# Linear attention's first head pair prepared inside neighbourhood attention, decay products on four row groups

## The chip, the cores and the metric

One core of a Trainium2 chip runs one program. The metric is the device time of one execution in microseconds (us). A second, profiled execution gives the rows below.

## What is computed

A first block of two layers over 2048 latent tokens and 256 context tokens (D = 1024), then a second block. One layer of the first block, cut to what matters here:

```python
(fx, fgx, nqx, nkx, nvx, ngx, gqx, gkx, gvx, ggx, zfx, zbx) = split(hx @ w_in[l])     # the same for the context
na_x = neighbourhood_attention(nqx, nkx, nvx, nkc, nvc, rpb[l])                       # 6 heads of 64
log_a = log_sigmoid(z @ w_alpha + b_alpha) / 16          # z: 16 columns, once forward, once backward
# gla_scan, chunks of 64 tokens, 4 heads, dk = 48 (padded to 64), dv = 96, both directions:
b = cumsum(log_a in the chunk); b_end = b[last]
q_dec, k_dec = q * exp(b), k * exp(-b)
o = tril(q_dec @ k_dec.T) @ v + q_dec @ state
state = exp(b_end) * state + (k * exp(b_end - b)).T @ v
x = x + gate * (concat(four_x, na_x, gla_x, each times silu(gate columns)) @ w_out[l])
```

The modulation (shift, scale, gate) of a layer is `silu(c) @ w_ada[l] + b_ada[l]`, for the latent and the context tokens.

## The kernel before

The program is a row of phases; each ends in a barrier of all engines, and the waits inside one are semaphores written out by hand. A layer of the first block has these:

- `cm` (`norm_project_cm`): norm, transpose, and the projection of twelve 128-column chunks, channels on partitions. Its 60 blocks (a chunk times 512 tokens, the fifth of each chunk 256) are 24 TensorE (PE) matmuls each: every float32 product is made of three fp32r products (`matmul3`, L72 to L74). The blocks n = 10 to 29 of chunks 2 to 5 are rotated for position (`Rotation`): one product L238 on PE after the next block, three VectorE (DVE) operations L248, L249, L251. In layer 0 `Modulation` is spread over the same blocks: GpSimd (POOL) loads 64 weight tiles of 256 KB into three buffers, DVE multiplies them into a sum in 64 steps of two operations (L335, L337), and after each of eight groups of eight steps PE reduces the sum (`reduce`, L307 to L316), which it reaches in its own order ahead of a block, waiting for `acc_ok`. Group j starts at block 9 + 6j with two steps in each of four blocks.
- `tm` (`project_tm`): four column chunks of 512, 512, 384, 384 columns times 16 or 18 token tiles, tokens on partitions, 24 matmuls a tile, ScalarE (ACT) evicts each (L940). Inside it `DecaySums` makes log_a and its running sums in 20 units (5 token segments times 2 head pairs times 2 directions), one after every third tile: one PE product of 16 contraction rows into one PSUM bank (L783), four ACT activations, two DVE operations, a store. The next segment's ranks are loaded into `z` by SyncE (SP) after the fourth unit's store.
- `four` (Fourier mix), then `na` (`neighbourhood_phase`): 18 (layer 0) or 16 (layer 1) query tiles times 6 heads, so NU = 108 or 96 units. In loop turn n DVE does `softmax_max(n + 2)` (L1285) and `probs_out(n)` (L1302), ACT does `exps(n + 1)` (L1339), on odd n `values_out` (L1345), and `tb` copies of unit n (L1357, L1359). PE does per pair of units the scores (L1215), transposes (L1227, L1233), values (L1245) and one transpose back (L1255).
- `gla` (`gla_phase`): head pairs hh = 0 and 1. SP loads the pair's running sums of both directions, k, v and q. ACT makes the exponentials of the chunk ends (`eb`, L1611), of the keys (L1614) and of the queries (L1618), DVE multiplies (`keys_decayed` L1540, `keys_to_end` L1544, `queries_decayed` L1551), PE transposes the keys back (L1452), ACT evicts them (L1625), PE makes the state updates of batch i (`states`, L1474), DVE chains them (`chain`, L1568), and a loop over the token tiles follows (products L1491, mask L1578, outputs L1503 and L1511). DVE's order is fixed: all six `prepare(0, n)` come ahead of `chain(0, 0)`. Pair 1 is prepared inside the loop of pair 0.
- `out` (`out_phase`): the output projection. Its weights come into the four buffers `wo.buf`, which are the decayed queries and keys of pair 0 before.

## Time and the profile before

| | us |
|---|---|
| median of 3 runs | 4718.71 (4718.05 to 4732.49) |
| the profiled execution | 4721.0 |
| its span | 4719.2 |
| PE busy | 4208.3 (89%) |
| DVE busy | 2202.5 (47%) |
| ACT busy | 1482.8 (31%) |
| POOL busy | 465.4 (10%) |

Times in the profile count from the start of the span. A matmul's end is modelled, and the matmuls of one row overlap, so a busy PE need not be at its peak; PEclk is the clock that PE was granted, 1.00 for 2.4 GHz and 0.50 for 1.2 GHz. In brackets stands how long the engine sat idle before an instruction, and what ended that. A float32 product counts as two MATMUL instructions. Layer 0's phases lie at about 64 to 430 (cm), 430 to 829 (tm), 829 to 943 (four), 943 to 1220 (na), 1220 to 1396 (gla), layer 1's na ends and its gla begins at about 2729.

### The profile page before, as it was taken

What the parts mean: (1) busy time and instruction counts of PE and PEld (TensorE: products, weight loads), DVE (VectorE), ACT (ScalarE), POOL (GpSimd) and SP (SyncE); (2) the same over time, 40 slices, a digit from 0 to 9 for tenths busy, and PEclk for the clock granted to TensorE, in tenths of its full rate; (3) what the DMA queues carried; (4) which work ended last, traced back from release to release, by engine and by line L of the source; (5) the groups of instructions that cost most, each with busy time, mean ns of one, the idle gap of its engine ahead of it and who ended that gap; (6) DMA issues with size and microseconds to landing.
All of it is one profiled execution on the core that took longest, in us unless ns stands there. A gap on an engine that the chain in (4) does not pass through costs nothing. (4 is left out here: it accounts for less than half of the span.)

```text
span 4719.2 us, 67376 instructions
## 1 busy us (share of the span) xinstructions
PE 4208.3 (89%) x25867; PEld 3358.5 (71%) x25867; DVE 2202.5 (47%) x4748; ACT 1482.8 (31%) x3341; POOL 465.4 (10%) x497
## 2 busy tenths in 40 slices
PE   7999999799669899999979956959999989979799
PEld 4777789577457778778857745847777767758687
DVE  5553111266656553111126665853831256657554
ACT  4001333156412220144316631431111257641211
POOL 3111000200000030000020000031420000100100
PEclk9999999999759999999989976979999999989899
DMA  4343121710325442212180043532111123346321
GB/s 179 118 132 112 72 72 54 262 42 13 127 101 200 171 151 69 94 72 72 58 273 14 14 151 125 219 148 78 63 65 64 61 84 118 96 156 256 116 75 64
DMA packets 230291, 520.88 MB, mean 110 GB/s; under 512 B 46587, under 2 KB 100747, under 8 KB 220627
## 3 DMA queue, kind: packets, MB, share of 16 engines
q1 hardware_dynamic: 206068, 434.47, 25.9%
q0 software_dynamic: 23904, 82.11, 4.8%
q8 instruction: 207, 3.39, 0.3%
q14 instruction: 112, 0.91, 0.1%
HBM read 320.07 MB, written 196.43 MB: 109 GB/s over the span
## 5 line engine op out<-in xcount | busy, mean ns | idle before, releaser
L72 PE MATMUL tm_tacc<-tm_tw_hi,hT_hi 128*128 128x384 f32 (+1 forms) x1120 | 418.6, 374 | 1.6 <-POOL tm_tw_lo L916 1.6
L73 PE MATMUL tm_tacc<-tm_tw_lo,hT_hi 128*128 128x384 f32 (+1 forms) x1120 | 413.4, 369 | 0.0
L74 PE MATMUL tm_tacc<-tm_tw_hi,hT_lo 128*128 128x384 f32 (+1 forms) x1120 | 413.3, 369 | 0.0
L72 PE MATMUL tz_tacc<-tz_tw_hi,hT_hi 128*128 128x512 f32 x896 | 359.8, 402 | 24.4 <-DVE tz_tw_lo L892 12.8
L72 PE MATMUL cm_acc<-hT_hi,cm_wb_hi 128*128 128x512 f32 (+1 forms) x912 | 362.0, 397 | 0.0
L73 PE MATMUL tz_tacc<-tz_tw_lo,hT_hi 128*128 128x512 f32 x896 | 356.1, 397 | 0.0
L74 PE MATMUL tz_tacc<-tz_tw_hi,hT_lo 128*128 128x512 f32 x896 | 356.1, 397 | 0.0
L74 PE MATMUL cm_acc<-hT_hi,cm_wb_lo 128*128 128x512 f32 (+1 forms) x912 | 344.0, 377 | 0.0
L73 PE MATMUL cm_acc<-hT_lo,cm_wb_hi 128*128 128x512 f32 (+1 forms) x912 | 343.5, 377 | 0.0
L804 DVE SCALAR_TENSOR_TENSOR tm_ds<-tm_dg,tm_ds 128x512 f32<-128x512 f32 (+1 forms) x40 | 25.6, 639 | 531.8 <-ACT tm_ds L798 531.8
L72 PEld LDWEIGHTS tm_tacc<-tm_tw_hi,hT_hi 128*128 128x128 f32 x1120 | 213.6, 191 | 56.5 <-ACT tm_tz L940 23.2
L74 PEld LDWEIGHTS tm_tacc<-tm_tw_hi,hT_lo 128*128 128x128 f32 x1120 | 213.3, 190 | 25.4
L73 PEld LDWEIGHTS tm_tacc<-tm_tw_lo,hT_hi 128*128 128x128 f32 x1120 | 213.6, 191 | 24.2
L72 PEld LDWEIGHTS tz_tacc<-tz_tw_hi,hT_hi 128*128 128x128 f32 x896 | 169.3, 189 | 78.8 <-POOL tz_tw_lo L916 17.8
L940 ACT ACTIVATE tm_tz<-tm_tacc 128x384 f32<-128x384 f32 (+1 forms) x140 | 75.8, 541 | 461.4 <-PE tm_tacc L74 426.0
L72 PE MATMUL out_acc<-out_w_hi,out_mT_hi 128*128 128x512 f32 x544 | 215.6, 396 | 0.0
L74 PE MATMUL out_acc<-out_w_hi,out_mT_lo 128*128 128x512 f32 x544 | 212.7, 391 | 0.0
L73 PE MATMUL out_acc<-out_w_lo,out_mT_hi 128*128 128x512 f32 x544 | 212.5, 391 | 0.0
L72 PEld LDWEIGHTS cm_acc<-hT_hi,cm_wb_hi 128*128 128x128 f32 x912 | 173.2, 190 | 41.5 <-issue 11.5
L724 ACT ACTIVATE cm_zo<-cm_acc 128x512 f32<-128x512 f32 (+1 forms) x57 | 32.2, 564 | 542.6 <-PE cm_acc L74 542.6
L73 PEld LDWEIGHTS cm_acc<-hT_lo,cm_wb_hi 128*128 128x128 f32 x912 | 173.4, 190 | 37.6 <-issue 7.5
L74 PEld LDWEIGHTS tz_tacc<-tz_tw_hi,hT_lo 128*128 128x128 f32 x896 | 169.5, 189 | 41.2
(370 smaller groups left out, 8801.2 us busy)
## 6 DMA issues: line engine op xcount, KB each, us to landing
scr_z<-tz_tz SPq DMA_DIRECT2D x112, 256.0 KB, 2.0
scr_zcm<-cm_zo SPq DMA_DIRECT2D x96, 256.0 KB, 2.0
scr_ztm<-tm_tz SPq DMA_DIRECT2D x68, 256.0 KB, 2.0
out_mx<-scr_mix SPq DMA_DIRECT2D x34, 512.0 KB, 3.6
out_gt<-scr_ztm SPq DMA_DIRECT2D x34, 512.0 KB, 4.5
scr_xres<-out_x POOLq DMA_DIRECT2D x34, 512.0 KB, 4.1
scr_z<-out_xn POOLq DMA_DIRECT2D x34, 512.0 KB, 4.7
cm_area<-in_w_ada POOLq DMA_DIRECT2D x64, 256.0 KB, 3.1
```

The source lines that it names most:

```text
L72: nc.tensor.matmul(out, ah, bh, start=start, stop=False)
L73: nc.tensor.matmul(out, ah, bl, start=False, stop=False)
L74: return nc.tensor.matmul(out, al, bh, start=False, stop=stop)
L724: act.activation(zo[n % 4][:, 0:b - a], acc[n % 4][:, 0:b - a], ACT.Copy).then_inc(ev_act, 1)
L804: nc.vector.scalar_tensor_tensor(s, g, 0.0, s, ALU.min, ALU.subtract)
L940: act.activation(zo[n % 3][:, 0:widths[c]], acc[n % 3][:, 0:widths[c]], funcs[c]).then_inc(ev, 1)
```

## The change

Four edits.

- A class `LinearInputs` (`pre`) holds, behind neighbourhood attention's own buffers, the four rows of pair 0, its k and q, `eb` and `ls`. SP loads them after the store of query tile 1. In the turns n = 24 onwards of `neighbourhood_phase` ACT makes one piece a turn (the chunk ends, then exponentials of 256 tokens), after `exps(n + 1)`; DVE multiplies the same piece two turns later, after `probs_out`. There are 38 pieces in layer 0 and 36 in layer 1.
- `gla_phase` no longer loads or prepares pair 0, except `keys_to_end(0, d)`, two DVE operations that now stand first. v is its first load, then the masks, then pair 1's four.
- `DecaySums` has ranks and weights on four row groups (partitions 0, 32, 64, 96) and four PSUM banks: the four products of a segment are issued together, once every fourth unit. The ranks of the next segment are loaded after the store of the first unit of a segment. All units move one tile later, so the first product is behind the first tile.
- `Modulation` starts at block 26 with a period of 4 blocks: three, three and two steps in blocks 27 + 4j, 28 + 4j and 29 + 4j; the reduction of group j stands ahead of block 31 + 4j (`reduced`, unchanged, asks for position 1 of the next period).

One more phase (`pre`) encloses the others, so one more barrier stands at a layer's end.

```diff
-        self.start, self.period = 9, 6
+        self.start, self.period = 26, 4
...
-        if p == 2 and 1 <= j <= self.NG:
+        if p == 1 and 1 <= j <= self.NG:
             self.row(dve, j - 1)
-        if 0 <= j < len(self.chunks) and p >= 2:
-            self.step(dve, j, 2 * p - 4)
-            self.step(dve, j, 2 * p - 3)
+        if 0 <= j < len(self.chunks) and p >= 1:
+            for k in range(3 * p - 3, min(3 * p, KC)):
+                self.step(dve, j, k)
...
-        self.z, self.wa, self.ba = P.sb("dz", [64, 512]), P.sb("dwa", [64, 256]), P.sb("dba", [128, 4])
+        self.z, self.wa, self.ba = P.sb("dz", [128, 512]), P.sb("dwa", [128, 128]), P.sb("dba", [128, 4])
...
-        self.bank = P.ps("dbank")
+        self.bank = [P.ps(f"dbank{j}") for j in range(4)]
...
-        self.at = {sum(tiles[:c]) + 3 * j: 5 * c + j for c in range(4) for j in range(5)}
+        self.at = {sum(tiles[:c]) + 3 * j + 1: 5 * c + j for c in range(4) for j in range(5)}
...
-            sp.wait_ge(self.g_mm, 4 * seg)
-        for d in range(2):
-            sp.dma_start(self.z[32 * d:32 * d + RANK, 0:w], rank_rows(self.io)[d, :, a:a + w]).then_inc(self.z_in, 16)
+            sp.wait_ge(self.g_mm, seg)
+        for j in range(4):
+            sp.dma_start(self.z[32 * j:32 * j + RANK, 0:w], rank_rows(self.io)[j % 2, :, a:a + w]).then_inc(self.z_in, 16)
...
-        if u % 4 == 3 and u < 19:
+        if u % 4 == 0 and u < 16:
...
     def pe(self, pe, u):
-        hh, d, a, w = self.place(u)
+        if u % 4:
+            return
         if u == 0:
-            pe.wait_ge(self.c_in, 48)
+            pe.wait_ge(self.c_in, 64)
         else:
             pe.wait_ge(self.g_ev, u)
-        pe.wait_ge(self.z_in, 32 * (u // 4 + 1))
-        self.nc.tensor.matmul(self.bank[:, 0:w], self.wa[32 * d:32 * d + RANK, hh * 128:(hh + 1) * 128],
-                              self.z[32 * d:32 * d + RANK, 0:w], start=True, stop=True).then_inc(self.g_mm, 1)
+        pe.wait_ge(self.z_in, 64 * (u // 4 + 1))
+        w = self.place(u)[3]
+        for j in range(4):
+            last = self.nc.tensor.matmul(self.bank[j][:, 0:w], self.wa[32 * j:32 * j + RANK, :], self.z[32 * j:32 * j + RANK, 0:w], start=True, stop=True)
+        last.then_inc(self.g_mm, 1)
...
-        act.wait_ge(self.g_mm, u + 1)
+        act.wait_ge(self.g_mm, u // 4 + 1)
...
-        act.activation(g, self.bank[:, 0:w], ACT.Identity, bias=self.ba[:, 2 * d + hh:2 * d + hh + 1]).then_inc(self.g_ev, 1)
+        act.activation(g, self.bank[u % 4][:, 0:w], ACT.Identity, bias=self.ba[:, 2 * d + hh:2 * d + hh + 1]).then_inc(self.g_ev, 1)
...
+                    if i == 2:
+                        pre.load(sp, io)
...
+                    if 0 <= n - first - 2 < len(pre.pieces):
+                        pre.dve(dve, n - first - 2)
...
+                    if 0 <= n - first < len(pre.pieces):
+                        pre.act(act, n - first)
...
-                for hh in range(2):
-                    sp.dma_start(qd[hh][0][:, :], decay_sums(io, hh, 0)).then_inc(b_in[hh][0], 16)
-                    sp.dma_start(k[hh][:, :], io["zcm"][10 + hh, :, :]).then_inc(k_in[hh], 16)
-                    sp.dma_start(qd[hh][1][:, :], decay_sums(io, hh, 1)).then_inc(b_in[hh][1], 16)
-                    if hh == 0:
-                        sp.dma_start(v[:, :, :], io["ztm"][:, 1024 + D_NA:TM].rearrange("(t p) c -> p t c", p=128)).then_inc(m["v_in"], 16)
-                    sp.dma_start(q[hh][:, 0:LQ], io["zcm"][8 + hh, :, 0:LQ]).then_inc(q_in[hh], 16)
-                    if hh == 0:
-                        for cc in range(2):
-                            sp.dma_start(mask[64 * cc:64 * cc + 64, :, :],
-                                         io["gla_mask"][64 * cc:64 * cc + 64, :, 64 * cc:64 * cc + 64]).then_inc(m["cst_in"], 16)
+                sp.dma_start(v[:, :, :], io["ztm"][:, 1024 + D_NA:TM].rearrange("(t p) c -> p t c", p=128)).then_inc(v_in, 16)
+                for cc in range(2):
+                    sp.dma_start(mask[64 * cc:64 * cc + 64, :, :],
+                                 io["gla_mask"][64 * cc:64 * cc + 64, :, 64 * cc:64 * cc + 64]).then_inc(m["cst_in"], 16)
+                sp.dma_start(qd[1][0][:, :], decay_sums(io, 1, 0)).then_inc(b_in[0], 16)
+                sp.dma_start(k[:, :], io["zcm"][11, :, :]).then_inc(k_in, 16)
+                sp.dma_start(qd[1][1][:, :], decay_sums(io, 1, 1)).then_inc(b_in[1], 16)
+                sp.dma_start(q[:, 0:LQ], io["zcm"][9, :, 0:LQ]).then_inc(q_in, 16)
...
-                    pe.wait_ge(m["qd_ok"], 2 * (hh + 1))
+                    if hh:
+                        pe.wait_ge(m["qd_ok"], 2)
...
-                nc.vector.memset(ls[:, :], math.log(GDK ** -0.5)).then_inc(m["ls_ok"], 1)
+                for d in range(2):
+                    keys_to_end(0, d)
...
-                for n in range(6):
-                    prepare(0, n)
+                dve.drain()
...
-                act.wait_ge(m["ls_ok"], 1)
-                exp_keys(0, 0)
-                exp_keys(0, 1)
-                exp_queries(0, 0)
                 keys_out(0, 0)
-                exp_queries(0, 1)
...
+class LinearInputs:
+    W = 256
+    def __init__(self, P, nc):
+        self.nc = nc
+        self.sums_in = [P.sem(f"sums{d}_in") for d in range(2)]
+        self.keys_in, self.queries_in, self.exp_ok, self.ls_ok = P.sem("keys_in"), P.sem("queries_in"), P.sem("exp_ok"), P.sem("ls_ok")
+    def place(self, P, LQ):
+        self.LQ = LQ
+        self.rows, self.eb, self.ls = self.behind(P)
+        self.k, self.q = [self.nc.alloc_sbuf_tensor(f"{P.name}_{n}0", [128, LT], F32, side="right") for n in "kq"]
+        self.pieces = []
+        for d in range(2):
+            self.pieces += [("ends", d, 0)] + [("keys", d, a) for a in range(0, LT, self.W)] + [("queries", d, a) for a in range(0, LQ, self.W)]
+    def behind(self, P):
+        right = lambda n, shape: self.nc.alloc_sbuf_tensor(f"{P.name}_{n}", shape, F32, side="right")
+        return [right(f"row{j}", [128, LT]) for j in range(4)], right("eb", [128, 2, 2, NCH]), right("ls", [128, 1])
+    def load(self, sp, io):
+        sp.dma_start(self.rows[0][:, :], decay_sums(io, 0, 0)).then_inc(self.sums_in[0], 16)
+        sp.dma_start(self.k[:, :], io["zcm"][10, :, :]).then_inc(self.keys_in, 16)
+        sp.dma_start(self.rows[1][:, :], decay_sums(io, 0, 1)).then_inc(self.sums_in[1], 16)
+        sp.dma_start(self.q[:, 0:self.LQ], io["zcm"][8, :, 0:self.LQ]).then_inc(self.queries_in, 16)
+    def act(self, act, j):
+        what, d, a = self.pieces[j]
+        b, e = self.rows[d], self.rows[2 + d]
+        if what == "ends":
+            act.wait_ge(self.sums_in[d], 16)
+            act.wait_ge(self.ls_ok, 1)
+            bc = b[:, :].rearrange("p (c t) -> p c t", t=CH)
+            act.activation(self.eb[:, 0, d, :], bc[:, :, CH - 1] if d == 0 else bc[:, :, 0], ACT.Exp, scale=1.0 / 16)
+            act.drain().then_inc(self.exp_ok, 1)
+        elif what == "keys":
+            act.activation(e[:, a:a + self.W], b[:, a:a + self.W], ACT.Exp, scale=-1.0 / 16)
+            act.drain().then_inc(self.exp_ok, 1)
+        else:
+            act.activation(b[:, a:a + self.W], b[:, a:a + self.W], ACT.Exp, scale=1.0 / 16, bias=self.ls[:, 0:1]).then_inc(self.exp_ok, 1)
+    def dve(self, dve, j):
+        what, d, a = self.pieces[j]
+        if what == "ends":
+            return
+        if j == 1:
+            dve.wait_ge(self.keys_in, 16)
+            dve.wait_ge(self.queries_in, 16)
+        dve.wait_ge(self.exp_ok, j + 1)
+        x, y = (self.rows[2 + d], self.k) if what == "keys" else (self.rows[d], self.q)
+        self.nc.vector.tensor_tensor(x[:, a:a + self.W], y[:, a:a + self.W], x[:, a:a + self.W], ALU.mult)
...
-        self.buf = [P.sb(f"buf{j}", [128, LT]) for j in range(4)]
+    def __init__(self, P, pre):
+        self.buf = pre.behind(P)[0]
...
+    with phase(nc, f"pre{l}") as Q:
+        pre = LinearInputs(Q, nc)
+        with phase(nc, f"nain{l}") as P:
+            na = Neighbourhood(P, last)
+            fourier_phase(nc, l, io, keep, na)
+            pre.place(P, LX if last else LT)
+            neighbourhood_phase(nc, l, io, keep, na, pre)
+        with phase(nc, f"wo{l}") as P:
+            wo = OutputWeights(P, pre)
+            gla_phase(nc, l, io, keep, wo, pre)
```

## Rows read from the trace of the kernel before

**Rows 1.** Busy time by phase, PE, PEld, DVE, ACT, POOL, granted clock, DMA share, GB/s.
```profile
437.00:841.00 404.00, 387.98 (x1784) 326.96 (x1783) 63.88 (x83) 148.35 (x202) 16.39 (x16) 0.97 0.21 77
943.00:1220.00 277.00, 266.60 (x2622) 193.97 (x2622) 177.76 (x400) 167.41 (x451) 0.00 (x0) 0.97 0.08 27
1220.00:1400.00 180.00, 114.15 (x1928) 98.19 (x1928) 109.60 (x303) 45.41 (x108) 0.00 (x0) 0.59 0.33 121
```

**Rows 2.** Timeline, layer 0, start of gla: start, duration, engine, instruction, [idle before].
```profile
1219.80 0.32 SPq L1419 DMA_DIRECT2D wo_buf<-scr_branch  x1
...
1226.20 0.26 ACT L1611 ACTIVATE gla_eb<-wo_buf 128x36 f32<-128x36 f32 x1 [10.98 <-DMA wo_buf<-scr_branch]
...
1231.63 2.56 DVE L1544 TENSOR_TENSOR gla_kd<-wo_buf,gla_eb 128x2304 f32<-128x2304 f32 x1
...
1234.25 4.10 PE L1452 MATMUL gla_bank<-ident,gla_kd 128*128 128x128 f32 x18 [18.65 <-DVE gla_kd L1544]
...
1244.00 3.53 PE L1474 MATMUL gla_bank<-gla_v,gla_kt 64*64 64x96 f32 x160 [0.53 <-ACT gla_kt L1625]
1244.33 5.03 DVE L1551 TENSOR_TENSOR wo_buf<-gla_q,wo_buf 128x2304 f32<-128x2304 f32 x2 [5.02 <-DMA gla_q<-scr_zcm]
...
1249.27 13.04 DVE L1568 SCALAR_TENSOR_TENSOR gla_S<-gla_S,gla_eb,gla_bank 128x96 f32<-128x96 f32 x40
...
1252.52 1.88 PE L1474 MATMUL gla_bank<-gla_v,gla_kt 64*64 64x96 f32 x40 [4.99 <-DVEq L1571]
```

**Rows 3.** Timeline, layer 1, start of gla.
```profile
2734.21 0.26 ACT L1611 ACTIVATE gla_eb<-wo_buf 128x36 f32<-128x36 f32 x1 [9.69 <-DMA wo_buf<-scr_branch]
...
2756.39 9.75 DVE L1568 SCALAR_TENSOR_TENSOR gla_S<-gla_S,gla_eb,gla_bank 128x96 f32<-128x96 f32 x30
```

**Rows 4.** ACT's groups by form in layer 0's na: busy, mean ns, idle before.
```profile
L1357 ACT ACTIVATE na_pt<-na_tpb 128x256 f32<-128x256 f32 x108 | 41.5, 384 | 86.8 <-PE na_tpb L1233 86.8
...
L1339 ACT ACTIVATE na_s<-na_s,na_st 128x256 f32<-128x256 f32 x12 | 6.0, 499 | 0.0
```

**Rows 5.** Timeline, layer 0's na, one pair of units.
```profile
1053.51 1.78 PE L1215 MATMUL na_sp<-nain_k,nain_q 64*128 64x512 f32 x12
1053.61 0.38 ACT L1357 ACTIVATE na_pt<-na_tpb 128x256 f32<-128x256 f32 x1 [0.63 <-PE na_tpb L1233]
...
1056.24 0.38 ACT L1357 ACTIVATE na_pt<-na_tpb 128x256 f32<-128x256 f32 x1 [1.12 <-PE na_tpb L1233]
```

**Rows 6.** Timeline of PE in tm, around one decay product.
```profile
509.72 0.40 PE L73 MATMUL tm_tacc<-tm_tw_lo,hT_hi 128*128 128x512 f32 x1
509.96 0.39 PE L74 MATMUL tm_tacc<-tm_tw_hi,hT_lo 128*128 128x512 f32 x1
510.39 1.09 PE L783 MATMUL tm_dbank<-tm_dz,tm_dwa 16*128 16x512 f32 x2
511.41 0.50 PE L72 MATMUL tm_tacc<-tm_tw_hi,hT_hi 128*128 128x512 f32 x1
```

**Rows 7.** The decay products' tile: instructions, duration min, median, max.
```profile
L783 PE MATMUL tm_dbank<-tm_dz,tm_dwa x80: 374/587/1189, 435.2 to 2325.9; 16*128 16x512 f32 x64, 16*128 16x256 f32 x16
```

**Rows 8.** Waits in tm, layer 0: us, times, longest.
```profile
PE tm_dbank L783 <- DMA tm_dz<-scr_branch: 12.4, 3, 8.0
```

**Rows 9.** Waits in cm, layer 0.
```profile
PE cm_msums L307 <- DVEq L341: 5.1, 3, 3.7
...
PE cm_ntp L238 <- DVE cm_zo L692: 3.3, 2, 2.5
```

**Rows 10.** Granted clock after two waits of PE, columns as in rows 1.
```profile
246.00:255.00 9.00, 6.56 (x14) 2.80 (x15) 4.23 (x7) 0.00 (x0) 0.00 (x0) 0.62 0.15 59
683.00:691.00 8.00, 7.53 (x21) 6.23 (x22) 0.00 (x0) 0.00 (x0) 0.00 (x0) 0.57 0.06 21
```

**Rows 11.** Timeline, DVE in cm, a modulation step that waited.
```profile
407.08 1.42 DVE L337 SCALAR_TENSOR_TENSOR cm_area<-cm_area,cs 128x512 f32<-128x512 f32 x2 [2.08 <-DMA cm_area<-in_w_ada]
```

**Rows 12.** DVE's groups in cm, the rotation's last operation.
```profile
L251 DVE TENSOR_TENSOR cm_zo<-cm_zo,cm_ntp 128x512 f32<-128x512 f32 x16 | 11.0, 688 | 1.2
```

More of the change, by code:

```diff
@@ L757, in ranks @@
         if seg:
-            sp.wait_ge(self.g_mm, 4 * seg)
-        for d in range(2):
-            sp.dma_start(self.z[32 * d:32 * d + RANK, 0:w], rank_rows(self.io)[d, :, a:a + w]).then_inc(self.z_in, 16)
+            sp.wait_ge(self.g_mm, seg)
+        for j in range(4):
+            sp.dma_start(self.z[32 * j:32 * j + RANK, 0:w], rank_rows(self.io)[j % 2, :, a:a + w]).then_inc(self.z_in, 16)
     def load(self, sp):
         l, io = self.l, self.io
-        sp.dma_start(self.wa[:, :], io["w_alpha"][l:l + 1, :, :].rearrange("a p n -> p (a n)")).then_inc(self.c_in, 16)
+        self.ranks(sp, 0)
+        for hh in range(2):
+            sp.dma_start(self.wa[64 * hh:64 * hh + 64, :], io["w_alpha"][l:l + 1, :, hh * 128:(hh + 1) * 128].rearrange("a p n -> p (a n)")).then_inc(self.c_in, 16)
         sp.dma_start(self.ba[:, :], io["b_alpha"][l:l + 1, :, :].rearrange("a p n -> p (a n)")).then_inc(self.c_in, 16)
         sp.dma_start(self.start[:, :], io["chunk_start"][:, 0:512]).then_inc(self.c_in, 16)
-        self.ranks(sp, 0)
     def store(self, sp, u):
@@ L1182, in neighbourhood_phase @@
         NPT = NA_H // 2
+        first = 4 * NA_H
         def key_tiles(i):
@@ L1374, in gla_phase @@
         mask = P.sb("mask", [128, 2, CH], I32)
-        ls = P.sb("ls", [128, 1])
-        q = [P.sb(f"q{j}", [128, LT]) for j in range(2)]
-        k = [P.sb(f"k{j}", [128, LT]) for j in range(2)]
+        ls = pre.ls
+        q, k = P.sb("q", [128, LT]), P.sb("k", [128, LT])
         v = P.sb("v", [128, NT, GH * GDV])
-        qd = [wo.buf[0:2], [P.sb(f"qd1{d}", [128, LT]) for d in range(2)]]
-        kd = [wo.buf[2:4], [P.sb(f"kd1{d}", [128, LT]) for d in range(2)]]
+        qd = [pre.rows[0:2], [P.sb(f"qd1{d}", [128, LT]) for d in range(2)]]
+        kd = [pre.rows[2:4], [P.sb(f"kd1{d}", [128, LT]) for d in range(2)]]
         kt = [P.sb(f"kt{d}", [128, NT, 128]) for d in range(2)]
         ke = [kd[1], [P.sb(f"ke{d}", [128, LT]) for d in range(2)]]
-        eb = P.sb("eb", [128, 2, 2, NCH])
+        eb = pre.eb
         S = P.sb("S", [128, 2, NCH, GDV])
@@ L1404, in steps_needed @@
             return max(order[0].index(2 * n + 1), order[1].index(2 * n))
-        names = ("cst_in", "v_in",
-                 "ls_ok", "exp_q", "exp_k", "qd_ok", "kte_ok", "kt_mm", "kt_ev", "u_mm", "s_ok", "a_mm", "a_ok", "o_mm", "o_ok")
+        names = ("cst_in",
+                 "exp_q", "exp_k", "qd_ok", "kte_ok", "kt_mm", "kt_ev", "u_mm", "s_ok", "a_mm", "a_ok", "o_mm", "o_ok")
         m = {n: P.sem(n) for n in names}
-        b_in = [[P.sem(f"b{hh}{d}_in") for d in range(2)] for hh in range(2)]
-        q_in, k_in = [[P.sem(f"{n}{hh}_in") for hh in range(2)] for n in ("q", "k")]
+        b_in = [P.sem(f"b{d}_in") for d in range(2)]
+        q_in, k_in, v_in = P.sem("q_in"), P.sem("k_in"), P.sem("v_in")
         o_out = [P.sem(f"o_out{j}") for j in range(2)]
@@ L1546, in keys_to_end, with queries_decayed, prepare @@
                                             eb[:, hh, d, :, None].to_broadcast([128, NCH, CH]), ALU.mult).then_inc(m["kte_ok"], 1)
-                def queries_decayed(hh, d):
-                    dve.wait_ge(m["exp_q"], 2 * hh + d + 1)
-                    dve.wait_ge(q_in[hh], 16)
-                    nc.vector.tensor_tensor(qd[hh][d][:, 0:LQ], q[hh][:, 0:LQ], qd[hh][d][:, 0:LQ], ALU.mult).then_inc(m["qd_ok"], 1)
-                def prepare(hh, n):
+                def queries_decayed(d):
+                    dve.wait_ge(m["exp_q"], d + 1)
+                    dve.wait_ge(q_in, 16)
+                    nc.vector.tensor_tensor(qd[1][d][:, 0:LQ], q[:, 0:LQ], qd[1][d][:, 0:LQ], ALU.mult).then_inc(m["qd_ok"], 1)
+                def prepare(n):
                     if n in (0, 2):
-                        keys_decayed(hh, n // 2)
+                        keys_decayed(n // 2)
                     elif n in (1, 3):
-                        keys_to_end(hh, n // 2)
+                        keys_to_end(1, n // 2)
                     elif n in (4, 5):
-                        queries_decayed(hh, n - 4)
+                        queries_decayed(n - 4)
                 def chain(hh, i):
@@ L1603, in _ @@
                         elif hh == 0:
-                            prepare(1, n - 3)
+                            prepare(n - 3)
             @block.scalar
@@ L2840, in first_layer @@
                            [512, 512, 384, 384], [ACT.Silu] * 2 + [ACT.Copy] * 2, tiles, decays=DecaySums(P, nc, l, io, tiles))
-    with phase(nc, f"nain{l}") as P:
-        na = Neighbourhood(P, last)
-        fourier_phase(nc, l, io, keep, na)
-        neighbourhood_phase(nc, l, io, keep, na)
-    with phase(nc, f"wo{l}") as P:
-        wo = OutputWeights(P)
-        gla_phase(nc, l, io, keep, wo)
-        out_phase(nc, l, io, keep, wo)
+    with phase(nc, f"pre{l}") as Q:
[8 more added lines that the diff above has]
+            gla_phase(nc, l, io, keep, wo, pre)
+            out_phase(nc, l, io, keep, wo)
 def program(nc, io):
```

21 lines of the change are left out of this document (10 added, 11 removed).

## The prediction

> **What bounds the kernel now.** I read the page first (PE busy nearly everywhere, the granted clock below full only in a few slices), then a table of busy time by phase, then timelines at the places that the diff touches, and the waits last. In the table [rows 1] three kinds of phase are to be seen. tm and na belong to PE: 388.0 busy of 404.0 us and 266.6 of 277.0, at a clock of 0.97. There, what PE no longer does is gained, and work of DVE or ACT costs nothing as long as PE doesn't wait for it. gla belongs to nobody: PE 114 and DVE 110 of 180 us, clock 0.59. That is a chain of waits, so its start has to be read instruction by instruction [rows 2]. SP issues the first load at 1219.80; ACT gets the running sums at 1226.20; DVE does keys (2.56 us an operation) for both directions and then waits 5.02 us for q, the last of the loads, at 1244.33, because its order puts both queries' multiplications ahead of the first chain. The chain, which everything behind it needs, starts at 1249.27, 29.5 us after the first load. PE had its state updates under way at 1244.00. Layer 1 does the same, with the chain at 2756.39 [rows 3].
>
> **The change, gla.** Of the head, what stays is: two `keys_to_end` (2 x 2.56), transposes, evictions, and v. DVE starts at once, so the second is done at 1219.9 + 5.1 = 1225.0; PE's transposes take 4.10 us for a direction [rows 2] at the low clock, so the keys are back at 1222.5 + 8.2 = 1230.7, evicted at about 1231.5. v is now the first load. Before, the sums of one direction (128 x 2304 x 4 bytes, 1152 KB) were there at 1226.20, and six more such pieces (k, the other sums, v as three, q) at 1244.33: 6912 KB in 18.1 us, 382 KB/us. v alone is 3456 KB, 2304 KB more than the first load was, so it lands at 1226.2 + 6.0 = 1232.2, and is what is late next. The first batch of updates is 40 of 160 instructions, 0.9 us at the pace of row 1244.00, 1.88 at that of row 1252.52 [rows 2]; I take 1.6 with the semaphore. The chain starts at 1234.0, 15.3 us earlier; in layer 1 at 2734.2 + 6.0 + 1.6 = 2741.8, 14.6 earlier. Pair 1 isn't in the way: its four loads follow v at 3.0 us each, done at about 1245, its exponentials 2 to 3 us behind, and DVE wants the first of them only in turn 3 of the loop, some 29 us after the chain's start. The masks, for which DVE waits ahead of the chain, are 64 KB behind v. Below, the gain is 12 us a layer, from the state updates themselves (1244.00 to 1232.2), above 16.5. I take **29 us** for both, a little less than 29.9.
>
> **na takes the work over.** ACT gets 38 and 36 pieces. The same engine's operation on 128 x 256 takes 384 ns (copy) and 499 ns (exponential) [rows 4]; the chunk ends 0.26 us each [rows 2]. In a pair of units ACT is idle 0.63 and 1.12 us ahead of its copies, and both waits are for PE [rows 5]; over the phase it is idle (277 - 167)/108 = 1.0 us a unit [rows 1]. A piece with its drain, 0.5 to 0.7, fits. DVE's part is 256/2304 of 2.56 us, 0.28, 0.35 with fixed cost; DVE is idle (277 - 178)/108 = 0.9 us a unit. Its tight place is `softmax_max` of the odd unit, for which the next scores wait. The loads, 4.7 MB at 382 KB/us, take 12 us and more and go out at about turn 15; a unit is 277/108 = 2.56 us, so turn 24 is 23 us later. They stand on SP's queue ahead of the store of query tile 2, whose buffer isn't wanted until tile 4, 12 units (31 us) on; no other SP work waits. So na's cost is **1 us**, from nothing to 0.4 us a piece (30 us) if the pieces come to stand in PE's way. Without the cover they would cost some 0.5 x 74 = 37.
>
> **tm, the decay products.** PE starts one matmul each 0.24 us; around the product the distance is 1.45 [rows 6], so one costs 1.21. Of the 20 a layer (80 instructions, 16 of them with 256 columns [rows 7]) the first stands ahead of the first tile, 15 are wide and four narrow (about 0.8): 18.2 + 3.2 = 21.4 us. The product also waits for its ranks: 12.4 us in three waits, 8.0 of which is the first [rows 8], where the weights' split is needed too and I count nothing. The two others, 4.4 us, go, since the ranks are loaded nine tiles earlier. Behind one of them PE's clock is 0.57 of full for 8 us, from 683 on [rows 10], the lower of its two levels for most of it: 0.43 x 8 = 3.4 us. Added are five groups. That products on different rows run together is seen in na: 832 columns for each of two heads take 1.78 us in 12 instructions [rows 5], where one of 512 columns alone takes 1.09 [rows 6]; one after the other would be 1664/512 x 1.09 = 3.5. For four groups of 32 rows there is no row. Below, a group costs what one product did, 1.21; above, three more behind it, 1.21 + 3 x 1.09 = 4.5. Nearest is the row of the pairs, so I take 1.5 (eight weight loads instead of two) and 1.0 for the narrow one: 7.0 a layer. Net 21.4 + 4.4 + 3.4 - 7.0 = 22.2, **44 us** for both. ACT and DVE do the same units at the same distance.
>
> The Trainium skill (TensorE: Matmul & The Clock Gate, the section on the measured speedup of packing) has four row tiles with 512 columns at 3.07 times, not four. By that, a group would take 4 x 1.09/3.07 = 1.42 where one takes 1.09, 0.33 more than the lower bound: 1.54 where I take 1.5, which changes the sum by less than 1 us. It is an estimate from that page; no run here shows it yet.
>
> **cm, the modulation.** Now PE waits 5.1 us for DVE's sums and 3.3 for evictions that stand behind modulation steps [rows 9], and the longest wait leaves a clock of 0.62 for 9 us [rows 10], 3.4: 11.8 us in all. After, the steps stand behind the rotation, but not wholly. Group 0 shares blocks 27 to 29 with it: from the end of block 27 and the rotation product behind it (1.2, like a decay product) DVE has three rotations of three operations of 0.69 [rows 12], eight steps of 1.5 (one is 1.42 and a drain [rows 11]) and an eviction: 1.2 + 6.2 + 12.0 + 0.7 = 20 us. PE has until the reduction three blocks of 24 matmuls at 0.24 (5.7, the narrow one 2.9, 5.7) and three rotation products, 18: a wait of 2. The last five steps of a group run in one go, 7.5 and 0.7, with waits for the weights of up to 2.08 [rows 11]; where one of the two blocks ahead of the reduction is narrow (groups 1, 5, 6), PE needs 8.6, so a wait of 1 each. Left are 5 us, the gain **7**; between -2, if these waits reach the 2 to 4 us behind which the clock falls, and 12.
>
> **Added beside.** One more barrier in each layer. A change of phase with two of them is what lies between ACT's last work in na and the load: 10.98 idle less 6.40 from the load's issue to its use, 4.6 [rows 2]. So one costs at most 4.6; I take 0.5, **1 us** for both. Three memsets of DVE and the constant for the queries lie in the shade.
>
> **Sum.** 44 + 29 + 7 - 1 - 1 = 78. The profiled execution took 4721.0 us, so 4643; it is 2.3 above the median of the runs shown, so 4641 there.
>
> **The rivals.**
> (1) The four products run one after another. For it: nothing here shows 32-row groups, and each product is two instructions on the same rows. Against it: the pairs in na. Four groups of 4.5 and one of 2.3 are 20.3 instead of 7.0 a layer, 27 in all: 4668.
> (2) The pieces get in PE's way in na. For it: ACT's program order is rigid, and the drain after a piece has no row of its own. Against: PE, not ACT, is waited for in both gaps. At 0.4 us for each of 74 pieces: 4641 + 29 = 4670.
> (3) The modulation's group sums come late. For it: five steps in a row with three buffers. At waits of 2 us or more in four groups, each followed by a low clock: 7 becomes -7, 4655.
> (4) gla's head is shorter but its gain is given back, because the loop's next wait (pair 1's exponentials, v behind other traffic) ends last. At half the 29: 4655.
> (5) Slower than before: the pieces let PE's clock fall. In na it is 0.97, and it falls elsewhere behind waits of 2.3 us [rows 10]. If PE waited so in the turns with pieces, 74 x 2.56 = 190 us would run at the lower level, up to 190 us more: some 4830. It decides from 78 + 14 = 92 of these 190 us on. Against: no wait of that length follows from pieces of 0.5.
>
> **Chances.** The forecast 0.56, rival 1 0.14, rival 2 0.11, rival 3 0.10, rival 4 0.06, rival 5 0.03. The forecast's own range comes from its bounds: all of them good (group 1.21, cm 12, gla 33, other waits of the first tile) is 4620; the range to 1 in 10 of rivals 1 and 2 ends at 4672. 0.3% is 14 us, which is what a measurement of this kernel can tell from no change. All but rival 5 and a piling up of 2, 1 and 3 are faster by more: faster 0.95, same 0.02, slower 0.03.
>
> **What would show it.** In gla, the first DVE row is `keys_to_end`, v lands 12 to 13 us after its issue and the chain starts 14 us after the phase; if it starts at 20 or more, the loads are to blame. In layer 0 na stays at 277 within 2, with PE's busy share; if PE waits for ACT's copies in turns 24 to 62, rival 2. In tm a product's distance appears five times a layer, 1.5 long; 4.5 is rival 1; no wait for ranks. In cm, waits of L307 and L312 in the second half only, below 2 us. The prediction is wrong by more than its range only if two of the parts fail, or if DMA traffic delays something that I took as hidden.

## The result and the profile after

The kernel after takes 4641.23 us (median of 4 runs, 4632.39 to 4649.88), the kernel before 4718.38 beside it (4 runs, 4711.15 to 4732.49). The ratio is 0.9833 with a 95% interval of 0.9802 to 0.9863: faster by 77 us, where 78 were forecast. An unchanged repeat, measured later, has 0.9813, 90 us less than before. The profiled execution of after is a short one, 4632.4 us with a span of 4630.5, and that of before took 4721.0, so the two traces differ by 88.7. Most of the 11 us between these two differences is not the change's, as the last experiment shows.

Busy time of after by phase, columns as in [rows 1]: tm, na and gla of layer 0.

```profile
417.60:791.40 373.80, 364.10 (x1768) 314.15 (x1768) 67.98 (x88) 149.64 (x203) 18.56 (x16) 0.99 0.21 74
911.00:1187.50 276.50, 265.34 (x2622) 192.72 (x2622) 189.46 (x435) 179.16 (x489) 0.00 (x0) 0.98 0.12 44
1187.50:1342.00 154.50, 104.82 (x1928) 90.93 (x1928) 97.41 (x297) 33.86 (x99) 0.00 (x0) 0.67 0.29 106
```

The tm window of [rows 1], 437 to 841, begins 9 us inside tm and ends 15 us behind it. This is before's tm from end to end:

```profile
427.70:826.00 398.30, 384.25 (x1768) 323.16 (x1768) 68.15 (x88) 149.64 (x203) 18.28 (x16) 0.97 0.19 69
```

In tm PE is busy 20 us less and the phase is 24.5 us shorter; na is as long as in [rows 1], although DVE and ACT each work 12 us more there; gla is shorter. The timeline of after from the start of gla in layer 0 shows the head that [rows 2] showed of before:

```profile
1187.50 0.37 SPq L1429 DMA_DIRECT2D gla_v<-scr_ztm  x1
1187.54 5.03 DVE L1553 TENSOR_TENSOR gla_kd<-nain_row,nain_eb 128x2304 f32<-128x2304 f32 x2 [3.34 <-PEq L79]
...
1190.16 6.96 PE L1460 MATMUL gla_bank<-ident,gla_kd 128*128 128x128 f32 x36 [6.82 <-DVE gla_kd L1553]
...
1201.19 6.01 PE L1482 MATMUL gla_bank<-gla_v,gla_kt 64*64 64x96 f32 x164 [4.07 <-DMA gla_v<-scr_ztm]
1203.21 3.84 DVE L1577 SCALAR_TENSOR_TENSOR gla_S<-gla_S,nain_eb,gla_bank 128x96 f32<-128x96 f32 x12 [9.61 <-PE gla_bank L1482]
```

DVE starts with `keys_to_end`, the transposes follow, and then PE stands still for v, which lands 13.7 us after its issue (12.4 forecast). The chain starts 15.7 us after the phase's first load, where it took 29.5 [rows 2]. Layer 1 has the chain at 2667.28, 13.5 us after the load:

```profile
2653.81 0.37 SPq L1429 DMA_DIRECT2D gla_v<-scr_ztm  x1
...
2667.28 2.95 DVE L1577 SCALAR_TENSOR_TENSOR gla_S<-gla_S,nain_eb,gla_bank 128x96 f32<-128x96 f32 x9 [7.36 <-PE gla_bank L1482]
```

PE in tm around a group of decay products, which answers to [rows 6]:

```profile
501.17 0.39 PE L74 MATMUL tm_tacc<-tm_tw_hi,hT_lo 128*128 128x512 f32 x1
501.49 1.14 PE L787 MATMUL tm_dbank<-tm_dz,tm_dwa 16*128 16x512 f32 x8
502.56 0.50 PE L72 MATMUL tm_tacc<-tm_tw_hi,hT_hi 128*128 128x512 f32 x1
```

From the matmul ahead to the one behind it is 1.39 us. Less the 0.24 that PE takes for each matmul, the group of eight instructions costs 1.15, less than the 1.21 which one product of two instructions cost in [rows 6]. (That one was a slow one, with a short idle time ahead of it; most of before's have a distance of 1.37 or 1.38.) The waits of PE in after, first in cm of layer 0 and then in its tm (line, waited for: us, times, longest):

```profile
PE cm_msums L307 <- DVEq L341: 2.6, 2, 2.4
...
PE cm_msums L316 <- DVEq L341: 0.7, 1, 0.7
```
```profile
PE tm_tacc L72 <- DVE tm_tw_lo L896: 4.8, 1, 4.8
PE tm_tacc L72 <- POOL tm_tw_lo L920: 3.7, 7, 0.7
```

Of cm's 5.1 and 3.3 [rows 9] 3.3 are left. In tm the 12.4 us for the ranks [rows 8] are gone, and 8.5 us for the weights' split stand in their place.

**The lengths of the phases.** From each trace I took the last eviction of cm and of tm, na's first scores and its last output, the chain's first step and gla's last output, and the last residual sum of layer 1's output phase. The table gives the stretches between them in us (the Fourier phases, layer 0's output phase with layer 1's cm, and layer 1's output phase aren't in it), for before, for after (its first profile and that of an unchanged repeat) and for the three parts of the change alone, whose runs come next.

| stretch | before | after | after, repeat | modulation alone | decays alone | linear inputs alone |
|---|---|---|---|---|---|---|
| to cm's end, layer 0 | 427.7 | 417.6 | 418.0 | 420.0 | 424.2 | 428.6 |
| tm, layer 0 / 1 | 398.3 / 374.9 | 373.8 / 353.4 | 374.2 / 354.2 | 394.3 / 375.4 | 373.7 / 353.7 | 399.7 / 374.1 |
| na, layer 0 / 1 | 273.3 / 258.5 | 273.4 / 259.5 | 274.9 / 258.9 | 274.5 / 258.5 | 274.7 / 258.6 | 274.7 / 260.6 |
| na's end to chain, 0 / 1 | 32.8 / 30.6 | 19.0 / 17.1 | 19.1 / 17.5 | 33.1 / 30.8 | 33.0 / 30.9 | 19.1 / 17.1 |
| chain to gla's end, 0 / 1 | 144.6 / 128.3 | 135.7 / 125.4 | 139.1 / 119.3 | 135.3 / 124.2 | 134.9 / 129.7 | 133.0 / 129.5 |
| all behind layer 1 | 1614.9 | 1617.6 | 1615.9 | 1624.4 | 1620.9 | 1622.4 |

### The profile page after: what moved, and what is told of

It reads as the page before. It is cut to its first block and busy times, and to the rows that moved or that the text cites. A ratio compares the mean times of both kernels' runs of the same rounds, so it can differ in the third digit from the quotient of the medians.

```text
span 4630.5 us, 67546 instructions
## 1 busy us (share of the span) xinstructions
PE 4152.1 (90%) x25867; PEld 3327.7 (72%) x25867; DVE 2207.5 (48%) x4810; ACT 1488.3 (32%) x3403; POOL 465.2 (10%) x497
## 5 line engine op out<-in xcount | busy, mean ns | idle before, releaser
L72 PE MATMUL tz_tacc<-tz_tw_hi,hT_hi 128*128 128x512 f32 x896 | 359.4, 401 | 24.9 <-DVE tz_tw_lo L896 12.4
L74 PEld LDWEIGHTS tm_tacc<-tm_tw_hi,hT_lo 128*128 128x128 f32 x1120 | 211.3, 189 | 25.4
```

What stands on the lines that cost most here:

```text
L72: nc.tensor.matmul(out, ah, bh, start=start, stop=False)
L74: return nc.tensor.matmul(out, al, bh, start=False, stop=stop)
```

## The experiments

**The three parts, each alone.** Each kernel is the one before with only those parts of the diff that concern it. The first:

```diff
-        self.start, self.period = 9, 6
+        self.start, self.period = 26, 4
```

> The kernel before with the modulation's new schedule alone (start 26, period 4). My theory: the waits of PE for DVE and the low clock behind the longest of them go, one wait of some 2.5 us stays at the first reduction; cm ends 10 us earlier (417.2 instead of 427.3), the whole time falls by 10 (7 by the prediction's term). Rival 3 of the prediction (sums late behind the rotation): cm not shorter, the time up by 7. Third possibility: cm is 10 us shorter, but tm's start gives it back because the weights' split and the first product's constants are late; then the whole is within 3 us of before.

Measured: 4710.44 us beside 4723.81, ratio 0.9968 (0.9956 to 0.9980), 13 us less by the medians, 15 by the ratio with an interval from 9 to 21. cm ends at 427.7, 424.2 and 428.6 in the three traces with the old schedule (mean 426.8) and at 417.6 to 420.3 in the eleven with the new one (mean 419.3), so cm itself gives 7.5 us. Another 4 stand in tm (394.3 instead of 398.3), whose code is the same as before's: PE waits for ranks as there, 2.50 us ahead of 675.7 and 2.38 ahead of 747.3, but no low clock follows, where before's two such waits (2.31 and 2.04 us) left two stretches at the lower level. The windows, first of before, then of this kernel:

```profile
683.90:690.60 6.70, 6.70 (x19) 5.54 (x18) 0.00 (x0) 0.00 (x0) 0.00 (x0) 0.50 0.00 0
759.00:762.30 3.30, 3.30 (x12) 3.30 (x12) 0.00 (x0) 0.00 (x0) 0.00 (x0) 0.50 0.00 0
```
```profile
675.70:690.00 14.30, 14.30 (x75) 13.17 (x76) 1.92 (x2) 6.21 (x9) 0.00 (x0) 1.00 0.08 29
747.30:760.00 12.70, 12.70 (x72) 12.37 (x73) 1.12 (x2) 5.06 (x8) 0.00 (x0) 1.00 0.12 41
```

10 us at half the clock cost 5. Whether this goes with the new schedule or with the single execution isn't shown, and cm's 7.5 alone lie below the interval, so the rest of the 15 has no shown cause. Rival 3 falls.

The second has `DecaySums` of after: four row blocks, four banks, a group at every fourth unit, the ranks' earlier load.

> The kernel before with the grouped decay products (and the ranks' earlier load) alone. My theory: per layer 20 products of 1.2 us become 5 groups of 1.15 and the two waits for ranks with the low clock behind one of them go: 22 to 23 us a layer, the time falls by 44 to 48. Rival 1 of the prediction (the four run one after another, 4.5 a group): falls by 18. Rival: the Fourier phase gives back what tm gains, because it waits for something that tm's length does not move: falls by less than 40, with na's start earlier by less than tm's end.

Measured: 4674.46 us, ratio 0.9905 (0.9889 to 0.9920), 45 us less by the ratio. tm is 24.6 us shorter in layer 0 and 21.2 in layer 1, and the Fourier phase behind it is as long as before's (117.4 and 117.1 in layer 0), so nothing is given back there. Rival 1 falls.

The third has `LinearInputs` and all that goes with it.

> The kernel before with the first pair of linear attention made in pieces inside neighbourhood attention, alone. My theory: the chain starts 14 us sooner after the phase's start in each layer, na is as long as before, one barrier more a layer: the time falls by 27. Rival 2 (pieces in PE's way): na longer by 0.4 us a piece, the fall is nil. Rival 4 (the gain given back later in the loop): falls by 14. A third one, from the profile of after: the loop of gla also runs at a higher clock when it starts earlier; then gla is shorter by 22 a layer and the time falls by 40 or more in every execution. If instead the clock in the loop is a matter of the execution, the granted clock of gla's second half differs between executions of one and the same gla, in both directions.

Measured: 4693.21 us, ratio 0.9934 (0.9921 to 0.9946), 31 us less. The way to the chain is 13.7 and 13.5 us shorter, na is within 2.1 us of before in both layers. The three ratios multiplied give 0.9808; after has 0.9833 (0.9802 to 0.9863) and its repeat 0.9813 (0.9792 to 0.9834). Within what these runs can tell, some 10 us, the parts add up.

**Grouping without the waits.** This kernel is after with its 20 products a layer apart again, two of the four row blocks holding the next segment's ranks, so that they are still loaded early.

```diff
-        if u % 4:
-            return
...
-        for j in range(4):
-            last = self.nc.tensor.matmul(self.bank[j][:, 0:w], self.wa[32 * j:32 * j + RANK, :], ...)
+        j = 2 * (u // 4 % 2) + d
+        self.nc.tensor.matmul(self.bank[u % 4][:, 0:w], self.wa[32 * j:32 * j + RANK, hh * 128:(hh + 1) * 128], ...)
```

> The kernel after, but the 20 decay products of a layer stand apart again, one a unit, each behind an ordinary tile of PE; the four row blocks of the ranks serve as two buffers, so that the ranks are still loaded early and nothing waits for them. It prices the grouping apart from the waits. My theory: 20 products of 1.2 instead of 5 groups of 1.15, 15.6 to 16 a layer, no wait for ranks and no low clock behind one: 32 us slower than after, 4673. Rival: what the grouping gave came mostly from the waits for ranks and the clock behind them: less than 15 us slower than after. Rival on the other side: a wait for ranks comes back although they are loaded early (the queue is the reason): 40 or more slower than after.

Measured: 4674.50 us, ratio 0.9898 (0.9885 to 0.9911), where after has 0.9833 and its repeat 0.9813: 31 us slower than the one, 40 than the other. tm takes 392.7 and 374.7 us, 19 and 21 more than in after, which is 40 in all. One product, in this kernel's timeline of PE:

```profile
488.78 0.40 PE L74 MATMUL tm_tacc<-tm_tw_hi,hT_lo 128*128 128x512 f32 x1
489.11 1.12 PE L785 MATMUL tm_dbank<-tm_dz,tm_dwa 16*128 16x512 f32 x2
490.16 0.50 PE L72 MATMUL tm_tacc<-tm_tw_hi,hT_hi 128*128 128x512 f32 x1
```

Its distance is 1.38, that of four together 1.39. Twelve wide ones less at 1.15 and three narrow ones at 0.7 are 15.9 us a layer. Of the other 3 and 5 us, 1.6 is the matmul behind: after one product as after four, the tile's second matmul follows its first at 0.33 us instead of 0.23. The rest is accounted for in part only: in layer 1 the clock fell twice more, for 3.4 us each time (1.7 lost each), in layer 0 it didn't. The first of these falls came behind two waits for the split, of 0.54 and 0.59 us:

```profile
2155.34 0.45 PE L72 MATMUL tm_tacc<-tm_tw_hi,hT_hi 128*128 128x384 f32 x1 [0.54 <-POOL tm_tw_lo L917]
2157.61 0.45 PE L72 MATMUL tm_tacc<-tm_tw_hi,hT_hi 128*128 128x384 f32 x1 [0.59 <-POOL tm_tw_lo L917]
```
```profile
2159.30:2162.80 3.50, 3.50 (x12) 3.41 (x12) 0.00 (x0) 0.00 (x0) 0.00 (x0) 0.51 0.94 331
```

What I had not expected: nothing waits for ranks here, and still tm of layer 1 is as long as before's (374.7 and 374.9). PE's waits of layer 1's tm:

```profile
PE tm_tacc L72 <- POOL tm_tw_lo L917: 5.5, 9, 0.7
PE tm_tacc L72 <- DVE tm_tw_lo L893: 4.5, 1, 4.5
```

These 10.0 us stand where before has 12.5 for the ranks and 0.8 for the split, and the clock falls behind two waits in both. PE, sooner at the chunks' starts and with no product ahead of their first tile, waits there for the weights instead.

**The ranks' earlier load, undone.**

```diff
-        if u % 4 == 0 and u < 16:
+        if u % 4 == 3 and u < 19:
             self.ranks(sp, u // 4 + 1)
```

> The kernel after, with the ranks of the next segment loaded after a segment's fourth product is stored, as in the kernel before, instead of after its first. It prices the earlier load, from which I took 4.4 us of waits and 3.4 of low clock a layer. My theory in the prediction: the third and fourth load come late behind the narrower tiles, two waits of 2.3 us each with a low clock behind them, tm 8 us longer a layer, 16 in all. Rival, from the run with the products apart, whose tm in layer 1 was as long as the kernel before's although nothing waited for ranks: PE then waits at the chunks' starts for the weights' split instead, so that the early load gives little by itself: tm longer by less than 3 us a layer.

Measured: 4667.27 us, ratio 0.9887 (0.9870 to 0.9903). tm is 386.6 and 367.6 us long, 12.4 and 13.4 more than in the repeat of after: more than either theory gave. The rival, drawn from the run with the products apart, is refuted. PE's waits for ranks in layer 1 and the longest of them in its timeline:

```profile
PE tm_dbank L787 <- DMA tm_dz<-scr_branch: 8.0, 4, 3.3
```
```profile
2169.85 0.34 PE L74 MATMUL tm_tacc<-tm_tw_hi,hT_lo 128*128 128x384 f32 x1
2173.46 2.09 PE L787 MATMUL tm_dbank<-tm_dz,tm_dwa 16*128 16x512 f32 x8 [3.27 <-DMA tm_dz<-scr_branch]
2175.48 0.69 PE L72 MATMUL tm_tacc<-tm_tw_hi,hT_hi 128*128 128x384 f32 x1
```

There are four waits where before had two behind its first, two of about 1 us new and two of some 3 us instead of 2.0 to 2.4; and the group behind this one runs at 1.2 GHz, 2.09 us instead of 1.14. In each layer the clock falls behind both of the 3 us waits. Why the waits are longer (a segment is four loads now and not two, and PE has fewer products on its way there) I didn't take apart. So grouping makes the early load urgent: with the products apart tm was 5.6 us shorter than before's in layer 0, where before's low clock cost 5, and 0.2 in layer 1; with the group the early load gives 13 us a layer.

**How much room ACT has in na.** One more exponential of 256 columns and a drain ahead of each piece that computes one, into a scratch buffer (36 and 34 pieces, 70 in all; the expectation says 72); in a second kernel three more, range(3).

```diff
+        if what != "ends":
+            for i in range(1):
+                act.activation(self.more[:, :], b[:, a:a + self.W], ACT.Exp, scale=-1.0 / 16)
+                act.drain()
```

> The kernel after, with one more exponential of 256 columns and a drain on ACT ahead of each piece (into a scratch buffer, 72 in all over both layers; what it computes is not used). It asks how much room ACT has in neighbourhood attention. In the turns with pieces ACT is idle 0.68 us ahead of each copy of the transposed probabilities, and a piece takes 0.41 to 0.50. My theory: 0.41 more each still fits, na longer by at most 3 us a layer, the whole by at most 5. Rival (pieces are already at the edge): each added one shows in full, 0.41 x 72 = 30 us slower than after.

Measured: 4641.63 us, ratio 0.9840 (0.9823 to 0.9858). na is 275.0 and 258.9 us, the repeat of after 274.9 and 258.9: nothing of it shows. The median is 15 us above the repeat's, but its trace has the difference outside na (5.5 us in gla's loop of layer 0 at a lower clock, 2.3 in cm).

> The kernel after, with three more such exponentials and drains on ACT ahead of each piece (not used either). 3 x 0.41 = 1.23 us a piece, of which 0.68 fits: 0.55 a piece is left, 20 us in each layer's na, 40 in all, and more if PE's clock falls for it (rival 5's mechanism: then the granted clock of na drops from 0.98 and na becomes longer by over 40 us a layer). Rival: the copies can wait much longer without PE noticing, since its buffers run two units ahead: less than 10 us in all.

Measured: 4677.15 us, ratio 0.9919 (0.9901 to 0.9936), 51 us more than the repeat of after; na is 25.4 and 23.6 longer, 49 in all, 0.70 a piece (0.55 expected). The windows of na and of its turns with pieces, and PE's waits in these turns, of this kernel:

```profile
911.00:1214.70 303.70, 275.15 (x2622) 193.48 (x2622) 190.45 (x436) 220.84 (x597) 0.00 (x0) 0.97 0.11 40
975.00:1180.00 205.00, 186.63 (x1842) 133.13 (x1840) 132.35 (x279) 164.64 (x447) 0.00 (x0) 1.00 0.04 13
```
```profile
PE na_tpb L1240 <- ACT na_pt L1371: 18.0, 33, 1.0
```

Here ACT's copies are what PE waits for, 33 times, and the clock stays full in these turns, 1.00: what is below it lies at na's start. So rival 5's mechanism didn't come about here, though shorter waits were followed by a low clock in the kernel with the products apart. The edge lies between one and three added exponentials.

**What is late next in gla.** v in eight loads, in the order in which the state updates want the tiles:

```diff
-                sp.dma_start(v[:, :, :], ...).then_inc(v_in, 16)
+                for i, parts in enumerate(v_parts):
+                    for a, b in parts:
+                        sp.dma_start(v[:, a:b, :], ...).then_inc(v_in[i], 16)
```

> The kernel after, with the load of v cut by token tiles in the order in which the state updates want them (tiles 16, 17, 0 and 15 first, then 1, 2, 13, 14, then 3 to 5 and 10 to 12, the rest last), with a semaphore for each part. In after, PE waits 4.1 us for v, and the transposed keys are evicted 3.3 us before v is there. My theory: v is what is late, so the chain starts 3.3 us earlier in each layer, na's end to chain 15.7 instead of 19.0, and the whole is 6 to 7 us shorter than after. Rival: the keys' copies on ACT or the chain's own entry end last anyway: less than 1 us a layer. Rival: eight loads instead of one take SP's queue and engines longer, and a later part is late in its turn: head shorter, but the chain's second or third batch waits, nothing gained.

Measured: 4635.98 us, ratio 0.9829 (0.9813 to 0.9845), not to be told from after. na's end to chain is 17.8 and 17.0, only 1.3 and 0.5 less. Its timeline:

```profile
1191.23 4.30 SPq L1433 DMA_DIRECT2D gla_v<-scr_ztm  x8
...
1195.57 1.29 SPq L1435 DMA_DIRECT2D gla_mask<-in_gla_mask  x2
...
1200.50 1.88 PE L1487 MATMUL gla_bank<-gla_v,gla_kt 64*64 64x96 f32 x80 [1.01 <-ACT gla_kt L1638]
...
1205.72 0.54 DVE L1582 SCALAR_TENSOR_TENSOR gla_S<-gla_S,nain_eb,gla_bank 128x96 f32<-128x96 f32 x2 [8.38 <-DMA gla_mask<-in_gla_mask]
```

PE begins its updates as soon as the keys are evicted, as hoped, but DVE stands at the wait for the masks, which are issued 4.3 us behind v's first part (0.4 in after). It is the prediction's "64 KB behind v" that becomes late. So the next two kernels move that wait behind the first four batches, where the masks are needed; one has v in parts too, the other v whole.

```diff
-                dve.wait_ge(m["cst_in"], 32)
                 for hh in range(2):
                     for i in range(4):
                         chain(hh, i)
+                    if hh == 0:
+                        dve.wait_ge(m["cst_in"], 32)
```

> The kernel after with v's load in parts, and DVE's wait for the masks moved from ahead of the first chain to behind its fourth batch, where the masked products need them. In the run with v in parts alone the first batch of state updates began 2 us sooner, but DVE then waited for the masks, which stand behind v on the queue. My theory: the masks were next in line; the chain now starts 4 to 5 us earlier than in after (14.5 us behind na's end instead of 19.0 in layer 0, 13 instead of 17 in layer 1), though the later batches wait a little for their parts of v; gla's end 3 us earlier a layer, the whole 6 us shorter than after, near what a measurement can tell. Rival: the later parts of v hold the chain's second and third batch so that its last step comes when it did.

Measured: 4627.92 us, ratio 0.9805 (0.9791 to 0.9820); na's end to chain is 14.0 and 14.4 us, 5.1 and 3.1 less than in the repeat of after. The chain's last step ahead of the loop also comes 5.1 and 3.1 us earlier (27.0 and 27.5 us behind na's end instead of 32.1 and 30.6), so the rival, later parts of v holding it up, is refuted. The row of the chain in its timeline:

```profile
1200.45 5.81 DVE L1582 SCALAR_TENSOR_TENSOR gla_S<-gla_S,nain_eb,gla_bank 128x96 f32<-128x96 f32 x18 [4.55 <-PE gla_bank L1487]
```

> The kernel after with DVE's wait for the masks moved alone, v in one load. The chain is bound by v there, so nothing changes: na's end to chain 19.0 and 17.3 us, within 0.3. If the masks, not v, were what the chain waited for, it starts earlier by up to the 1.2 us between the first batch's end and the chain's start.

Measured: 4629.41 us, ratio 0.9822 (0.9807 to 0.9837); 19.3 and 18.1 us, so the wait alone does nothing, as expected in layer 0; layer 1 is 0.8 above what was expected. The two moves together start the chain 8 us earlier over both layers, but the kernel's time (0.9805 beside 0.9822, intervals that overlap) doesn't show it beyond doubt. The first of the two has the lowest ratio of all; that it beats after isn't shown.

**The barrier.** Four more empty phases in each layer between na and gla:

```diff
+        for i in range(4):
+            with phase(nc, f"x{l}{i}") as X:
+                X.sem("s")
```

> The kernel after, with four more empty phases, each with one semaphore, between neighbourhood attention and linear attention in each layer, eight in all. It prices the barrier that the change adds, which I took as 0.5 us and bounded by 4.6. At 0.5 the gap from na's last DVE work to the chain grows by 2.0 us a layer, 4 in all; at the upper bound by 18 a layer, 37 in all; if the ends of phases are hidden behind GpSimd's own queue, by nothing.

Measured: 4643.92 us (4627.72 to 4648.74), ratio 0.9841 (0.9822 to 0.9860). DVE's first operation of gla in this kernel's timeline:

```profile
1188.30 5.03 DVE L1553 TENSOR_TENSOR gla_kd<-nain_row,nain_eb 128x2304 f32<-128x2304 f32 x2 [4.91 <-PEq L79]
```

The gap is 4.91 us where after has 3.34, so a barrier costs 0.39. na's end to chain grows by 1.7 and 1.5.

**The same loop at two clocks.** For the expectation on the clock in the repeat of after, whose kernel is unchanged:

> The kernel after, unchanged, so that the runs of this call have it beside them on the same chip. From na's last DVE work to the chain 19.0 us in layer 0 and 17.1 in layer 1, na 273.4 and 259.5 us, as in its first profile, within 0.5. If the clock in gla's loop is a matter of the execution, the stretch from the chain's start to gla's end, 135.7 and 125.4 us there, differs here by several us in one direction or the other, together with the granted clock of gla (0.67 and 0.71 there).

Measured: 4626.54 us (4619.51 to 4640.52), ratio 0.9813 (0.9792 to 0.9834). The head came out as in the first profile within 0.5, na of layer 0 was 1.5 longer (274.9), outside what I had expected of it; from chain to gla's end it took 139.1 and 119.3 us instead of 135.7 and 125.4. The extremes are in two other kernels with that same gla, one more exponential (first row) and four more barriers (second row); windows from the chain to gla's end in layer 0, columns as in [rows 1]:

```profile
1209.00:1354.00 145.00, 105.99 (x1856) 91.33 (x1848) 91.31 (x290) 28.34 (x88) 0.00 (x0) 0.62 0.20 75
```
```profile
1204.00:1333.50 129.50, 85.96 (x1855) 73.22 (x1848) 91.31 (x290) 28.35 (x88) 0.00 (x0) 0.76 0.23 84
```

The same instructions, DVE's and ACT's busy time equal to a hundredth, and 15.5 us between them: PE is granted 0.62 in the one and 0.76 in the other.

## Why the prediction was right, step by step

The forecast was 4641.0 and the result 4641.23; its mechanisms held. That the two numbers agree to 0.2 us is luck: the unchanged repeat took 4626.54, 90 us less than before beside it. The sizes of the terms, with what each measured:

- **tm, 44 forecast, 46 measured** (24.5 and 21.5). The products were worth 15.9 a layer and not 14.4. The group costs 1.15 and not 1.5 (1.7 more): the lower bound, which I had put at 1.21. The first product, which I had left out with the first wait, is saved too (1.2 more), and a single one costs 1.14 and not 1.21 (1.4 less). The slower matmul behind each of them, another 1.6, I had not seen. The Trainium skill (TensorE: Matmul & The Clock Gate, section "Measured speedup vs the span model") has 3.07 times for four row tiles at 512 columns; by that my estimate for the group was 1.54. Here the measurement decides otherwise: four products take the time of one, 1.39 and 1.38 by distance. The waits for ranks (4.4) did go. The clock behind them I had at 3.4 from one fall; in this trace of before there are two falls in each layer, worth 5.0 and 3.4, but with the modulation alone layer 0 had none, so this term changes from one execution to the next. What I left out is that PE then comes to the chunks' starts sooner and waits for the split: 8.5 us in layer 0 where nothing but 0.8 was. 4.8 of that stand against the 8.0 of the first wait for ranks, which I had counted at nothing, a gain of 3.2; the other 3.7 are a loss of 2.9. That these two nearly cancel is luck. All the terms together give about 3 us a layer more than was measured; part of it is that a short wait costs PE more than its idle time (0.59 idle, 0.75 by distance), the rest is open.
- **gla, 29 forecast, 27.4 measured** (13.8 and 13.6 less from na's end to the chain, the added barrier in it). v landed after 13.7 us in layer 0 and 12.3 in layer 1; 12.4 was worked out.
- **cm, 7 forecast, 7.5 measured** in cm itself, with a single long wait, 2.4 us at the first reduction, where 2 was worked out. The whole time of the kernel with this part alone fell by more, 9 to 21 us; what is beyond cm isn't explained.
- **na, 1 forecast, nothing to be told from zero**: 273.4 and 259.5 beside 273.3 and 258.5, and one more exponential for each piece would still be hidden. **Barriers, 1 forecast, 0.8 measured.**
- **Not forecast:** the Fourier phase between tm's end and na's first scores is 119.4 us in after and 117.1 in before; with the modulation alone it is 119.2, with the other two parts alone 117.4 and 117.0. Only the clock's low stretches there differ (41 us of them with the modulation alone, 24 in before, but 38 with the decays alone). That it belongs to the new modulation isn't shown: the run with the ranks late has the new modulation and 117.2.

The rivals: (1) serial products: refuted by the group's row. (2) pieces in PE's way: refuted, and the price of the edge is known, 0.70 a piece at three more. (3) late sums: refuted, waits of 3.3 us in all. (4) gain given back: from the chain to gla's end layer 0 takes 129 to 145 us with the new inputs and 135 to 145 with the old ones, layer 1 119 to 133 and 124 to 130: nothing is given back that can be told from the loop's own scatter. (5) PE's clock in na: 0.98 after, 0.97 before.

The sum against the two profiled executions (88.7) is 11 too small, and most of that is the clock: the loop in gla of layer 0 was 8.9 us shorter in after, yet old code has it at 134.9 and 135.3 too in other executions.

## What to carry to other kernels

Small products that leave most of the array's rows unused are worth grouping by rows, but price what the group needs at once: its operands' load becomes urgent as PE gets there sooner, and an early load that gave little for scattered products gave 13 us a layer for grouped ones. Work of a waiting phase can move into a phase that another engine bounds, as long as each piece fits the engine's idle time per turn; measure that edge by adding dummy pieces. When one wait is taken away, list in the engine's program order what it waits for next: here v, then the masks, both behind a wait placed earlier than its use.

## What the runs showed of the hardware that I had not expected

- Four float32 products of 16 rows and 512 columns on four row blocks take PE 1.15 us between its other matmuls, one takes 1.14.
- One and the same loop (gla from the chain on, layer 0) took 129.3 to 144.6 us in eight traces with the same code for it, with PE's granted clock from 0.76 to 0.62. The whole time scatters with it: the four runs of after have spans of 4630.5 to 4648.0 us and mean clocks of 0.941 to 0.935. What decides at which level an execution passes through that loop is not settled; no run varied it on purpose. It limits what can be told here: medians of kernels that should differ by less than 5 us lie between 4627 and 4644.
- Eight smaller loads of v keep SP's queue for 4.3 us, where one takes 0.37, so the masks, next on it, are issued 4 us later.
- The length of a wait alone doesn't tell whether the clock falls. 33 waits of up to 1.0 us in 205 us of na left it at 1.00, and so did waits of 2.50 and 2.38 us in tm; behind waits of 0.54 and 0.59 us it fell to 0.51 for 3.4 us, behind one of 2.31 us to 0.50 for 6.7. What decides isn't shown.
